# A depthwise convolution of block two as 32x32-tiled fp32 products

## The reference, cut to what matters

```python
CONV_CH, CONV_WIDTH = 256, 31
def conv_mixer(u, w, b, gn_g, gn_b):
    a, gt = jnp.split(u, 2, axis=-1)
    z = a * jax.nn.sigmoid(gt)
    zp = jnp.pad(z, ((0, 0), (CONV_WIDTH - 1, 0), (0, 0)))
    y = depthwise_conv(zp, w) + b          # y[s, c] = sum_n zp[s + n, c] * w[n, c] + b[c]
    ...                                    # layer norm within groups of 64 channels, swish
```

## Time and profile before

| | |
|---|---|
| median of 3 runs | 1082.59 us (1082.26 to 1083.15) |
| the profiled execution's own time | 1084.47 us |
| its span from first to last instruction | 1081.5 us |
| PE / DVE / ACT busy | 98% / 73% / 65% of the span |
| mean granted TensorE clock | 1.000 |
| stretch from step 20 to the first output product | 807.57 to 845.15 us of the span |

### The profile page before, as it was taken

How to read it: one execution, slowest core, us unless ns; L and a number is a source line. 1 busy time by engine, 2 the same in 40 slices (tenths; PEclk the granted TensorE clock), 3 DMA queues, 4 the chain that set the end, 5 groups by cost and what they waited for, 6 DMA issues and landing times.

```text
span 1081.5 us, 21673 instructions
## 1 busy us (share of the span) xinstructions
PE 1058.9 (98%) x8032; PEld 959.8 (89%) x8032; DVE 792.7 (73%) x1315; ACT 697.6 (65%) x1260; POOL 61.4 (6%) x100
## 2 busy tenths in 40 slices
PE   8999999999999999999999999999999999999998
PEld 8999788899999899978899999999989878888886
DVE  5856667877777896676787777775987778568985
ACT  6675666655555786467665555566966556457774
POOL 1002500000000000250030000000000000000000
PEclk9999999999999999999999999999999999999999
DMA  7643124565555464502366656553543335768991
GB/s 265 188 153 116 42 71 167 185 192 181 190 189 178 118 198 140 175 18 79 118 207 188 185 189 188 180 175 125 164 126 115 97 136 205 288 228 299 333 363 56
DMA packets 50665, 184.15 MB, mean 170 GB/s; under 512 B 5664, under 2 KB 5824, under 8 KB 50464
## 3 DMA queue, kind: packets, MB, share of 16 engines
q1 hardware_dynamic: 49680, 180.00, 50.9%
q0 software_dynamic: 912, 3.16, 0.9%
HBM read 182.09 MB, written 1.05 MB: 169 GB/s over the span
## 4 chain that ended last, share of the span: by engine, by line
PE 86%; DVE 6%; ACT 5%; DMA 2%; issue 1%; DVEq 0%; SPq 0%; ACTq 0%
PE bank L1871 24%; PE bank L1872 23%; PE bank L1873 23%; PE bank L1972 4%; DMA ring<-wtiles 1%; PE bank L1956 1%; DVE x L2721 1%; DVE act L2704 1%; PE bank L1037 1%; PE bank L2165 1%; DVE w L2680 1%; PE bank L2036 1%; DVE sq L2712 1%; ACT w L2355 1%; PE bank L956 1%
## 5 line engine op out<-in xcount | busy, mean ns | idle before, releaser
L2680 DVE TENSOR_TENSOR w<-ring,w 128x1024 fp32r<-128x1024 f32 x240 | 293.2, 1225 | 97.9 <-ACT w L2355 97.2
L1871 PE MATMUL bank<-act,w 128*128 128x256 f32 x1136 | 324.5, 286 | 2.8 <-DVE w L2680 2.6
L1872 PE MATMUL bank<-act,w 128*128 128x256 f32 x1136 | 321.4, 283 | 0.0
L1873 PE MATMUL bank<-act,w 128*128 128x256 f32 x1136 | 321.3, 283 | 0.0
L2355 ACT ACTIVATE w<-ring 128x1024 fp32r<-128x1024 f32 x240 | 252.9, 1055 | 68.3 <-PE bank L1873 47.5
L1871 PEld LDWEIGHTS bank<-act,w 128*128 128x128 f32 x1136 | 217.6, 192 | 7.9 <-issue 3.7
L1872 PEld LDWEIGHTS bank<-act,w 128*128 128x128 f32 x1136 | 217.7, 192 | 1.7
L1873 PEld LDWEIGHTS bank<-act,w 128*128 128x128 f32 x1136 | 217.7, 192 | 0.0
L2990 DVE SCALAR_TENSOR_TENSOR region<-bank,pf,region 128x255 f32<-128x255 f32 (+1 forms) x176 | 84.8, 482 | 33.6 <-ACT region L2637 23.4
L1871 PE MATMUL bank<-w,hid 128*128 128x512 f32 x206 | 80.9, 393 | 0.0
L1872 PE MATMUL bank<-w,hid 128*128 128x512 f32 x206 | 80.6, 391 | 0.0
(11 more groups left out here) (474 smaller groups left out, 1978.0 us busy)
## 6 DMA issues: line engine op xcount, KB each, us to landing
ring<-wtiles SPq DMA_DIRECT2D x240, 512.0 KB, 3.6
ring<-etiles SPq DMA_DIRECT2D x33, 512.0 KB, 5.2
act_raw<-etiles SPq DMA_DIRECT2D x33, 512.0 KB, 5.0
sq<-etiles SPq DMA_DIRECT2D x22, 512.0 KB, 5.2
cst<-etiles SPq DMA_DIRECT2D x8, 512.0 KB, 4.9
region<-packp POOLq DMA_DIRECT2D x4, 512.0 KB, 4.5
cst<-consts SPq DMA_DIRECT2D x1, 1176.5 KB, 11.6
x<-xt SPq DMA_DIRECT2D x2, 512.0 KB, 5.8
```

The lines of the kernel that those rows point to most:

```text
L1871: t.matmul(out_, still[:, 0], moving[:, 0], start=first, stop=False)
L1872: t.matmul(out_, still[:, 0], moving[:, 1], start=False, stop=False)
L1873: return t.matmul(out_, still[:, 1], moving[:, 0], start=False, stop=last)
L2680: v.tensor_tensor(w_lo[:, s, :], ring[:, s, :], w_hi[:, s, :].bitcast(F32), ALU.subtract).then_inc(lo_ready, 1)
```

## The change

The tap tiles leave the ring (234 tiles are left) and the steps; the last token tiles move from u = 21, 22 to u = 20, 21, and the within-block products are issued between the products of tile 20. The DVE taps, the splits of c_z and the closing addition are removed. The tap weights come as 32x32 diagonal blocks in two DMAs of 512 KB from POOL's queue, into the places of `hid` and `thin`. All 62 taps run on PE as fp32 products of 32x32: row block r (32 partitions of channels) against column block q, where q says which half (j) and which of two neighbouring taps it is. So each bank of `CONV_BANKS` (one for each r) collects in its four 32-partition quarters four partial sums. ACT copies the four banks out (`conv_copy`), and eight products with `fold32` add the two sums of each half and put them in place (`conv_fold`); ACT adds the bias. The convolution parts stand at u = 23 to 26 and the first waits for `df_sm` 7; the lengths of the attention move to bank 7; L903 moves behind out_part(1).

```diff
-U_CONV, U_DQ, U_OG, U_DVA, U_GV, U_DVB, U_STEPS = 2, 6, 14, 16, 18, 21, 28
-TAP_TILES = 6
-U_TAPS = (20, 23, 24, 25, 26, 27)[:TAP_TILES]
+U_CONV, U_DQ, U_OG, U_DVA, U_GV, U_DVB, U_STEPS = 2, 6, 14, 16, 18, 20, 28
...
+PAIRS_OF_TAPS = (CW + 1) // 2
+CONV_STEPS = {23: (0, 5), 24: (5, 10), 25: (10, 13), 26: (13, PAIRS_OF_TAPS)}
+CONV_BANKS = (6, 0, 1, 5)
...
+            def conv_part(first, end):
+
+                if first == 0:
+                    pe.wait_ge(cz_ready, 2)
+                    pe.wait_ge(taps_in, 32)
+                    pe.wait_ge(st_copied, 2)
+                    pe.wait_ge(df_sm, 7)
+                    pe.wait_ge(u_evac, evacuated(U_DVB + 1))
+                for s in range(first, end):
+                    for turn_ in range(4):
+                        for r in range(4):
+                            q = (r + turn_) % 4
+                            j, tap = q // 2, 2 * s + q % 2
+                            if tap >= CW:
+                                continue
+                            rows_, outs = slice(32 * r, 32 * r + 32), slice(32 * q, 32 * q + 32)
+                            still = tap_parts[s // 8][rows_, s % 8 * P + 32 * q:s % 8 * P + 32 * q + 32]
+                            mm = t.matmul(bank[CONV_BANKS[r]][outs, 0:S], still, c_z[rows_, j, tap:tap + S],
+                                          start=s == 0, stop=tap + 2 >= CW)
+                if end == PAIRS_OF_TAPS:
+                    mm.then_inc(cp_done, 1)
+
+            def conv_fold():
+
+                pe.wait_ge(cp_copied, 4)
+                for j in range(2):
+                    for r in range(4):
+                        mm = t.matmul(bank[1][32 * r:32 * r + 32, j * S:(j + 1) * S], cc("fold32", j, 32), c_part[:, r, :],
+                                      start=True, stop=True)
+                mm.then_inc(cp_done, 1)
...
-                elif u in U_TAPS:
-                    if u == U_TAPS[0]:
-                        pe.wait_ge(cz_low, 2)
-                        pe.wait_ge(st_copied, 2)
-                    tile_in(n)
-                    for i in range(KD):
...
+                elif u in CONV_STEPS:
+                    conv_part(*CONV_STEPS[u])
...
-                        mm = lengths(bank[0][:, 2 * j:2 * j + 2], d_osq[:, j, :], ones[:, 0:1])
+                        if j == 0:
+                            pe.wait_ge(df_sm, 8)
+                        mm = lengths(bank[7][:, 2 * j:2 * j + 2], d_osq[:, j, :], ones[:, 0:1])
...
-            out_part(0)
+            out_part(0, (0,))
+            pe.wait_ge(cp_copied, 1)
+            pe.wait_ge(hn_std, 2)
+            out_part(0, (1,))
+            conv_fold()
             pe.wait_ge(hn_inv, 2)
-            pe.wait_ge(cy_ready, 2)
             for j in range(DFH):
                 spread(bank[4 + j // 2][:, j % 2 * S:j % 2 * S + S], o_inv[:, 2 * j:2 * j + 2]).then_inc(hn_row, 1)
+            out_part(1)
+            pe.wait_ge(cy_ready, 2)
             for j in range(2):
                 mm = t.matmul(bank[0][:, j * S:(j + 1) * S], bd64, c_y[:, j, :], start=True, stop=True)
             mm.then_inc(cm_done, 1)
-            out_part(1)
             out_part(2)
...
+            def conv_copy(r):
+
+                a.activation(c_part[:, r, :], bank[CONV_BANKS[r]][:, 0:S], ACT.Copy).then_inc(cp_copied, 1)
...
                 if u == U_STEPS - 1:
+                    act.wait_ge(cp_done, 1)
+                    conv_copy(0)
                     act.wait_ge(gla_mix, 1)
...
-                    a.activation(o_rms[:], bank[0][:, 0:2 * DFH], ACT.Sqrt, bias=eps, scale=1.0 / P).then_inc(hn_std, 1)
-                    a.activation(c_y[:, 1, :], bank[5][:, S:2 * S], ACT.Identity, bias=pb_("convb", 1)).then_inc(cy_ready, 1)
+                    a.activation(o_rms[:], bank[7][:, 0:2 * DFH], ACT.Sqrt, bias=eps, scale=1.0 / P).then_inc(hn_std, 1)
+                    for r in range(1, 4):
+                        conv_copy(r)
+                    act.wait_ge(cp_done, 2)
+                    for j in range(2):
+                        a.activation(c_y[:, j, :], bank[1][:, j * S:(j + 1) * S], ACT.Identity, bias=pb_("convb", j)).then_inc(cy_ready, 1)
...
         def second_pool(pool):
+            pool.wait_ge(tile_done, T2)
+            pool.dma_start(tap_parts[0][:], ctaps[0]).then_inc(taps_in, 16)
+            pool.wait_ge(lr_done, 1)
+            pool.dma_start(tap_parts[1][:], ctaps[1]).then_inc(taps_in, 16)
```

More of the change, by code:

```diff
@@ L173 @@
 BETWEEN = ((1, 6), (6, 11), (11, NGB))
-TAPS = [(j, w) for j in (1, 0) for w in range(CW)]
-PE_TAPS, DVE_TAPS = TAPS[:8 * TAP_TILES], sorted(TAPS[8 * TAP_TILES:], key=lambda tap: (tap[1], tap[0]))
-TAPS_AT = {9: 1, 10: 1, 17: 1, 19: 1, 23: 1, 24: 1, 25: 4, 26: 2}
 TURN_STEPS, VALUE_STEPS, LENGTH_STEPS = (20, 22, 24, 25), (21, 23, 25, 26), (26, 26, 26, 27)
+PAIRS_OF_TAPS = (CW + 1) // 2
+CONV_STEPS = {23: (0, 5), 24: (5, 10), 25: (10, 13), 26: (13, PAIRS_OF_TAPS)}
+CONV_BANKS = (6, 0, 1, 5)
 MIX_ORDER_2 = (0, 1, 4, 5, 6, 7, 2, 3)
@@ L187, in evacuated @@
 def evacuated(u):
-    return sum(i not in CONV_VALUES and i not in U_TAPS for i in U_TILES if i <= u)
+    return sum(i not in CONV_VALUES for i in U_TILES if i <= u)
 def columns(*widths):
@@ L317, in block_program @@
         gid = ctx.enter_context(nc.sbuf_tensor("gid", [P, NG], mybir.dt.int32))
+        places["hid"] = -(-nc.sbuf_base // 32) * 32
         hid_both, hid_hi, hid_lo = split("hid", 2, S)
         thin_both, thin_w_hi, thin_w_lo = split("thin", KD * 64)
-        cz_hi = hid_both[:].rearrange("p b q s -> p (b q s)")[:, 0:2 * (S + CW - 1)].rearrange("p (j s) -> p j s", j=2)
-        cz_lo = thin_both[:].rearrange("p b n -> p (b n)")[:, 0:2 * (S + CW - 1)].rearrange("p (j s) -> p j s", j=2)
+        assert nc.sbuf_base == places["hid"] + 4 * 2 * 1024 and 4 * S == KD * P
+        tap_parts = [nc.alloc_sbuf_tensor_at(f"taps{i}", [P, 1024], F32, offset=places["hid"] + i * 4096) for i in range(2)]
         last_both, last_hi, last_lo = (a_[..., 0:S] for a_ in (thin_both, thin_w_hi, thin_w_lo))
@@ L727, in later_scores, with within @@
                     first_scores(late)
-            between_tokens = {U_SCORES: later_scores}
+            def within(i):
+                if i == 4:
+                    within_rows()
+                if i == KD - 1:
+                    within_keys()
+            def conv_part(first, end):
[25 more added lines that the diff above has]
+                mm.then_inc(cp_done, 1)
+            between_tokens = {U_SCORES: later_scores, U_WITHIN: within}
             pe.wait_ge(packb_in, 16)
@@ L3150, in shape_constants @@
     put("onecol", np.tile(np.arange(33) == 1, (P, 1)))
+    put("fold32", np.concatenate([(i[:, None] // 64 == q) & (i[:, None] % 32 == np.arange(32)[None, :]) for q in range(2)], axis=1))
     put("halfcols", i[:, None] // 64 == np.arange(32)[None, :])
@@ L3223 @@
     ct, dvt = tiles(cu), token_tiles(dv)
-    taps = np.zeros((TAP_TILES, P, KD, P), np.float32)
-    for tap, (j, n) in enumerate(PE_TAPS):
-        taps[tap // KD, np.arange(P), tap % KD, np.arange(P)] = w["conv_w_2"][0][n, j * P:(j + 1) * P]
-    taps = taps.reshape(TAP_TILES, P, KD * P)
+    ctaps = np.zeros((P, PAIRS_OF_TAPS, 2, 2, 32), np.float32)
+    for n in range(CW):
+        for j in range(2):
+            ctaps[np.arange(P), n // 2, j, n % 2, np.arange(P) % 32] = w["conv_w_2"][0][n, j * P:(j + 1) * P]
+    ctaps = np.ascontiguousarray(ctaps.reshape(P, 2, 1024).transpose(1, 0, 2))
     second = dict(zip(U_TILES[:U_DVA], np.concatenate([tiles(gq), tiles(gk), ct[[0, 2, 1, 3]], tiles(dk), tiles(dq), tiles(gog)])))
     second.update(zip(U_TOKENS, np.concatenate([dvt[0:2], token_tiles(gv), dvt[2:4]])))
-    second.update(zip(U_TAPS, taps))
     parts += [np.stack([second[u] for u in U_TILES]), rows_of(w["w_out_2"][0])[list(MIX_ORDER_2)]]
```

59 lines of the change are left out of this document (6 added, 53 removed).

## The result

The changed kernel takes 1089.08 us (1086.42 to 1090.90, 7 executions), the kernel before beside it 1083.34 us (1082.26 to 1084.16, 7 executions): ratio 1.0049, 95% interval [1.0033, 1.0064]. It is slower by more than the 0.2% that can be told. The prediction was 1081.1 us, 0.14% faster. All of that is in or behind the changed stretch, and more: up to there this execution ran 1.85 us ahead (the third call of the scores starts at 811.22 where it started at 813.06).

The account below looks back on a forecast made before the run. TensorE (PE) was taken to bound the kernel, busy 98% of the span with 86% of the chain. Out_part(0) 2.5 us earlier, less 1.05 for the fold, gave -1.5 us: 1081.1 from the 1082.59 median; range 1077.5 to 1089.

Parts of the forecast that it names:

- step 2: The convolution's new form on PE: 496 records at 15.5 ns plus 0.8 us, 8.5 us; bounds 7.5 and 30.6 us.
- four entries: Going in and out of the tiled form in the convolution, 4 x 0.2 us.
- rival A: Convolution records come further apart; saving gone at 18.5 ns (10.0 us), 1086.8 us with eight tiles at once; chance 0.22.
- Rival C: PE slows after standing; first convolution part and L832 to L834 take +2.5 to +4 us, 1083.6 to 1085.1; chance 0.13.
- Step 3: With the tap tiles gone, PE stands for DVE: 3.8 us at the scores, 2.5 us before the convolution's first part.
- Step 4: Rest of the stretch: 0.6 us of waiting, out_part(0) 2.5 us earlier, 1.05 taken back by the fold, sum -1.5 us.
- the fold: Eight products of 128x32 by 256 columns on PE between out_part(0) and the spreads, 1.05 us with an entry.
- Step 5: Tap DMAs and removed c_z splits, costed at nothing: 1 to 2 us delay if uncovered, at most 0.8 us gained.
- Slower: Whole kernel above 1084.8 us; chance 0.28.

Follow-up runs that it names:

- the filled version: Changed kernel with row blocks 1 to 3 of the convolution begun ahead of both waits, row block 0 following; 1083.6 us, ratio 0.9999 to the kernel before.

## Why the prediction was wrong, point by point

**The clause that failed is step 2, the pace.** I took 15.5 ns and four entries for sixteen tiles from rows with four (64x64). It is 19.8 ns by the difference of two parts, 20.8 with the entry. At full clock the four parts take 3.32 + 3.32 + 2.05 + 1.92 = 10.6 us, 2.1 more than the 8.5 of the sum. That passes rival A's break-even of 10.0 us. The step from "four tiles work at once, nearly free" to "sixteen do as well" had no row; the runs show that it holds for eight (27 ns) and fails for sixteen. The check that I had named for this, over 18.5 ns and the prediction is wrong, is what the timeline shows. The Trainium skill ("TensorE: Matmul & The Clock Gate", section "Measured speedup vs the span model") gives a measured 10.6 times for sixteen tiles of 32x32, with 512 columns; 218 / 20.8 = 10.5 here, in long bursts of 256 columns, is close to it, and I hadn't used it. The smallest distance of about 25 ns between matmuls, which the prediction weighed from the same page of the Trainium skill (section "Wait — 56ns, not 53.3ns?"), does not hold over different tiles here: 20.8 ns with 256 columns, 10.7 with 64.

**Rival C came on top, not instead.** The step that failed here is that the sum priced PE's standing at full clock and kept the half clock as a case apart. The fall of the clock after the 3.58 us of standing made the first part 1.26 us longer; the scores and turns behind it took 1.2 us more as well, but DVE's chain covered that: the wait ahead of the convolution shrank from the forecast 2.5 to 1.46 us, and the part began at 823.65, the forecast 825.4 being 823.55 with this execution's lead. The experiment that keeps PE at work gives 1.13 us for all of it, less than the 2.5 to 4 of the rival, since part of the slow time lay inside waiting. The Trainium skill ("TensorE: Matmul & The Clock Gate", section "HAM oscillation — how this bites in real kernels") has such a fall after idling; the trace agrees (0.50 for 6.8 us), though the falls at 841 and 902 come where PE does not stand, and the one at 878 behind stands of 0.50 and 0.35 us.

**Step 3 held.** 3.8 us forecast at the scores, 3.58 measured; 2.5 at the convolution, 1.46 here, but 2.50 and 2.56 in the profiles with three row blocks and with two taps, where the scores kept their clock. The conclusion that the attention's chain eats most of the gain is what the run with two taps shows outright.

**Step 4:** the wait at out_part(0) was 0.70 (forecast 0.6), the fold 1.01 (1.05). The other products between the first part and out_part(0) took 0.9 us more than reckoned, a term that the prediction had at nothing beyond its four entries. Kernel before, timeline of PE, around a turn between two tap tiles:

```profile
830.65 0.49 PE L1972 MATMUL bank<-cst,region 128*128 128x128 f32 x3
830.90 0.36 PE L760 MATMUL bank<-hid,w 128*128 128x256 f32 x1
```

This turn took 0.25 us to the start of what follows, and takes 0.48 (834.14 to 834.62) between two parts. The other three groups took 2.42, 1.81 and 3.51 us and take 2.59, 1.99 and 3.83. So the same products cost about 0.2 us more each time they stand beside parts on 32x32 tiles, on top of the 0.2 us inside each part: going in and out once costs some 0.4 us, where the sum had 0.2. Another 0.3 us lie between out_part(0) and the measure's end. **Step 5 held:** ACT's waits for the ring are 1.52 and 1.16 us (1.54 and 1.35 before), and the 0.81 us at 785 is as it was.

**Sum.** Forecast -1.5; pace +2.1, first part at half clock +1.26, other products +0.9, start of the first part +0.1, wait +0.1, behind out_part(0) +0.26: +3.2, the measured 3.25. The fall near 902 in this profile adds 1.6. The median of the 7 (1089.08) lies 2.2 us over the profiled one at the same mean clock of 0.994, so not for more falls; the 1.85 us that the profiled execution ran ahead up to the stretch are about that much. The executions with 0.991 and 0.992 have further falls, which a profile of their own would have to place (the runs with rows outer and with masked(5) first show them at 847 and 905).

**Chances.** Slower had 0.28; A and C were listed as separate cases with a time each, while both together, 1081.1 + 2.1 + 1.1 and the 0.9 beside the parts, were given none. The range reached to 1089.0 and missed by 0.1 us.

## What to carry to other kernels

A burst on tiles that no row shows should be priced by the rows for the number of tiles that was seen, and the step beyond it kept as a separate doubt: up to eight tiles were free here, the next eight gave a factor of 1.4. When a change takes work off the bounding engine in the middle of a chain of other engines, look for independent work to put into the waits it opens (the filled version brought back 4.6 us of the stretch in its profile); the clock stayed up there too. A tiled burst is to be charged for going in and out, some 0.4 us each time here. And where a stand of some 3 us is forecast, what follows it is to be priced at half clock in the sum itself and not only as a rival.

## What the hardware showed that I had not expected

- fp32 records in sixteen 32x32 tiles start 20.8, 14.1 and 10.7 ns apart with 256, 128 and 64 columns; eight tiles with 256 columns 27 ns without and 29.0 with entry, in either arrangement.
- At half clock sixteen tiles lose less than half their pace: 160 records took 5.52 us (824.65 to 830.17, rows outer) instead of 3.33, eight tiles 4.45 instead of 2.32.
- The clock can fall to 0.50 where PE has not stood: for 3.4 us at 902, behind products of five columns, and at 841, near one-column products. At 902 this costs 1.6 us. In one execution of the unchanged kernel it fell at 878, behind stands of 0.50 and 0.35 us and four-column products, and in another, with the same rows, it did not.
- Ordinary products beside parts on 32x32 tiles take about 0.2 us longer, to the start of what follows, than beside tiles of 128x128 (0.48 for 0.25, 2.59 for 2.42, 1.99 for 1.81 us).
- With short records in sixteen tiles (64 and 128 columns) PE stands for 0.55 to 1.11 us in the convolution, put down to "issue".
